# A transformer step with expert-choice routing: expert tokens picked on chip by register-addressed copies instead of gathered from DRAM

## The reference

```python
x = x + g1 * (mix @ w_out)
h2 = rms_norm(x, norm2_g) * (1 + sc2) + sh2           # modulated, sc2/sh2 differ for context and latent
x = x + g2 * expert_choice(h2, w_router, w_gate, w_up, w_down)

def expert_choice(h, w_router, w_gate, w_up, w_down):
    C = EC_FACTOR * T // N_EXPERTS                    # 64 of 512, 16 of 128
    aff = softmax(h @ w_router)
    gsel, idx = top_k(aff.T, C)                       # each expert picks its tokens
    xs = h[idx]
    hid = silu(xs @ w_gate[e]) * (xs @ w_up[e])
    ye = hid @ w_down[e] * gsel
    return zeros.at[idx].add(ye)
```

## Time and profile before

| | us |
|---|---|
| Median of three runs | 1949.23 (1947.59 to 1951.15) |
| Profiled execution: span from the first to the last instruction | 1948.8 |
| Profiled execution: its own time beside the span | not given by the page |
| TensorE busy | 1717.8 (88%) |
| VectorE busy | 630.2 (32%) |
| ScalarE busy | 327.0 (17%) |
| GpSimd busy | 139.3 (7%) |
| Mean DMA rate over the span | 274 GB/s |

### The profile page before, as it was taken

The page is one execution under the profiler, slowest core; times in us unless marked ns, Lnnn a source line. Parts: engine busy times, 40 slices in busy tenths (PEclk is TensorE's granted clock), DMA queues, the critical chain, the costliest instruction groups (busy, mean ns, idle before and its releaser), DMA issues.

```text
span 1948.8 us, 60484 instructions
## 1 busy us (share of the span) xinstructions
PE 1717.8 (88%) x28403; PEld 1357.9 (70%) x28403; DVE 630.2 (32%) x1056; ACT 327.0 (17%) x667; POOL 139.3 (7%) x169
## 2 busy tenths in 40 slices
PE   4999988967998899898969998899499999898983
PEld 2555456547998889888845444755489988898883
DVE  2399277251111111010127975832411111010112
ACT  3100156320010101010030003542110101010001
POOL 2100000100000000000010000000000000000002
PEclk9999999988999999999979999999699999999997
DMA  9246540436999999999941643033499999999995
GB/s 360 84 173 236 196 162 1 170 143 239 384 388 399 388 398 399 388 399 387 394 161 55 221 167 139 13 119 130 147 386 389 393 395 399 387 400 389 399 388 211
DMA packets 154439, 534.70 MB, mean 274 GB/s; under 512 B 5937, under 2 KB 6354, under 8 KB 154386
## 3 DMA queue, kind: packets, MB, share of 16 engines
q1 hardware_dynamic: 139600, 484.99, 64.6%
q0 software_dynamic: 12320, 42.47, 7.5%
q10 hardware_dynamic: 2466, 6.50, 0.8%
HBM read 509.30 MB, written 24.64 MB: 274 GB/s over the span
## 4 chain that ended last, share of the span: by engine, by line
PE 57%; DMA 30%; DVE 8%; SPq 2%; ACT 2%; issue 1%; POOL 0%; ACTq 0%; POOLq 0%; DVEq 0%
DMA weight_ring<-in_w_gate_dram 24%; PE ps L760 17%; PE ps L527 14%; PE ps L666 7%; PE ps L777 6%; PE ps L564 3%; DMA weight_ring<-in_w_down_dram 3%; PE ps L457 2%; DVE neg_m L1264 2%; SPq L356 2%; PE ps L626 1%; DMA weight_ring<-in_conv_w_dram 1%; PE ps L790 1%; DVE weight_ring L1300 1%; PE ps L686 1%
## 5 line engine op out<-in xcount | busy, mean ns | idle before, releaser
L760 PE MATMUL ps<-v_sb,weight_ring 128*64 128x80 f32 x16384 | 614.0, 238 | 74.9 <-DMA weight_ring<-in_w_gate_dram 51.4
L760 PEld LDWEIGHTS ps<-v_sb,weight_ring 128*64 128x64 f32 x16384 | 599.1, 141 | 93.0 <-DMA weight_ring<-in_w_gate_dram 54.7
L777 PE MATMUL ps<-mix,weight_ring 128*64 128x80 f32 x8192 | 294.3, 233 | 7.5 <-DMA weight_ring<-in_w_down_dram 4.3
L777 PEld LDWEIGHTS ps<-mix,weight_ring 128*64 128x64 f32 x8192 | 286.5, 137 | 14.5 <-issue 10.1
L527 PE MATMUL ps<-mix,weight_ring 128*128 128x512 f32 (+1 forms) x1024 | 285.1, 439 | 1.3 <-DVE mix L1158 1.0
L527 PEld LDWEIGHTS ps<-mix,weight_ring 128*128 128x128 f32 x1024 | 155.1, 193 | 130.1 <-issue 128.8
L1426 DVE TENSOR_TENSOR mix<-mix,ps 128x320 f32<-128x320 f32 x64 | 28.3, 483 | 644.5 <-PE ps L760 644.5
L1186 DVE SCALAR_TENSOR_TENSOR weight_ring<-u_gate,conv_cols,weight_ring 128x655 f32<-128x655 f32 x240 | 195.3, 887 | 0.0
L666 PE MATMUL ps<-weight_ring,mix 128*128 128x512 f32 x320 | 140.2, 592 | 0.0
L1433 DVE SCALAR_TENSOR_TENSOR qk<-ps,gsel,gate 80x1024 f32<-80x1024 f32 x32 | 41.0, 1280 | 284.7 <-PE ps L790 284.7
L1564 POOL DMA_INDIRECT x_res<-qk,row_idx x32 | 46.2, 1444 | 972.2 <-DVE qk L1433 941.2
(11 more groups left out here) (183 smaller groups left out, 1178.0 us busy)
## 6 DMA issues: line engine op xcount, KB each, us to landing
weight_ring<-in_w_gate_dram SPq DMA_DIRECT2D x64, 2048.0 KB, 23.8
weight_ring<-in_w_up_dram SPq DMA_DIRECT2D x64, 2048.0 KB
weight_ring<-in_w_down_dram SPq DMA_DIRECT2D x64, 2048.0 KB, 26.5
weight_ring<-in_w_mod_dram SPq DMA_DIRECT2D x24, 2048.0 KB, 8.2
weight_ring<-in_w_in_dram SPq DMA_DIRECT2D x10, 2048.0 KB, 12.6
weight_ring<-in_w_out_dram SPq DMA_DIRECT2D x4, 2048.0 KB, 9.2
x_res<-x_tile POOLq DMA_DIRECT2D x10, 512.0 KB, 3.3
x_unit<-x_norm ACTq DMA_DIRECT2D x10, 512.0 KB, 2.6
```

The lines of the kernel that those rows point to most:

```text
L760: last = nc.tensor.matmul(ps[c * HALF:(c + 1) * HALF, 2 * (i % 2) + f // BLK, f % BLK * CAP:(f % BLK + 1) * CAP], w[:, kk, o:o + HALF], pi ...
L777: last = nc.tensor.matmul(ps[c * HALF:(c + 1) * HALF, 4 + d // BLK, d % BLK * CAP:(d % BLK + 1) * CAP], w[:, kk, o:o + HALF], hid[:, k, :] ...
```

## The change

`x_unit` and the gathers are gone. `h2_lo` and `h2_hi` write the modulated, transposed tile into `mix` at the tile's own columns, so that after the router stage `mix` holds all 640 tokens. Each expert's 80 columns are copied from there, one token a copy (128 partitions by 8 elements), at an address held in a register: GpSimd copies tokens 0 to 39, ScalarE 40 to 79. The registers are loaded in groups of eight. For expert 0 the indices are read from the top-k tile as each round ends; for the others SP stores all indices to DRAM and loads them back as one row on partition 0. `picked_t` has two buffers. TensorE's loop is written for two experts a turn; ScalarE's is unrolled. Some waits of the router stage go with the store of `x_unit` and with the single `h2_t`. `hid`, `silu_g` and `result_t` move out of `mix`; the final norm's gain is loaded into `x_norm`.

```diff
+TOP_ROUNDS = CAP // 8
+PICK_SPLIT = 40
+PICK_LOAD = 8
...
+        picked_t = v_sb[:, 0:2 * KD * CAP].rearrange("p (b k n) -> p b k n", b=2, k=KD)
...
+        def picks_of(engine, e, at, n):
+            src = top_i[0:1, at:at + n] if e == 0 else pick_row[:, e * CAP + at:e * CAP + at + n]
+            return nc.values_load_multi_w_load_instructions(
+                src, engines=[engine], min_val=0, max_val=(N_LAT if at < CAP_LAT else N_CTX) - 1,
...
+        def picked_row(j, pick):
+            rows = mix[:, :, N_CTX:N_TOK] if j < CAP_LAT else mix[:, :, 0:N_CTX]
+            return rows[:, :, bass.ds(pick, 1)]
...  (SP, between expert 0's loads and the loop)
+                sp.wait_ge(*top_round.at(l, TOP_ROUNDS))
+                sp.dma_start(picks, top_i).then_inc(picks_stored.sem, 16)
+                sp.wait_ge(*picks_stored.at(l, 1))
+                sp.dma_start(pick_row, picks.rearrange("(a e) n -> a (e n)", a=1)).then_inc(picks_loaded.sem, 16)
...  (TensorE)
-                def picked_transposes(e):
-                    pe.wait_ge(*gathered.at(l, e + 1))
...
-                def gate_up(e):
-                    pe.wait_ge(*picked_ready.at(l, e + 1))
+                def gate_up(e, b):
+                    pe.wait_ge(*picked_lo_ready.at(l, e + 1))
+                    pe.wait_ge(*picked_hi_ready.at(l, e + 1))
...
-                    picked_transposes(e + 1)
-                    down(e)
-                    result_transposes(e)
+                with nc.Fori(0, EXPERTS // 2, engines=[mybir.EngineType.PE], hint_back_edge=True) as pair:
+                    for b in range(2):
+                        gate_up(2 * pair + b, b)
+                        pe.wait_ge(*result_taken.at(l, 2 * pair + b + 1))
+                        down(2 * pair + b)
+                        result_transposes(2 * pair + b)
...  (ScalarE)
-                        act.wait_ge(*unit_stored.at(l, i))
...
-                    act.dma_start(x_unit[tokens(OUT_TILES[i]), :], x_norm[:]).then_inc(unit_stored.sem, 16)
...
-                    if i > 0:
-                        act.wait_ge(*logits_done.at(l, i))
...
+                def pick_hi(e):
+                    for at in range(PICK_SPLIT, CAP, PICK_LOAD):
+                        if e == 0:
+                            act.wait_ge(*top_round.at(l, at // 8 + 1))
+                        elif e == 1 and at == PICK_SPLIT:
+                            act.wait_ge(*picks_loaded.at(l, 1))
+                        for j, pick in enumerate(picks_of(mybir.EngineType.Activation, e, at, PICK_LOAD), at):
+                            last = nc.scalar.activation(picked_t[:, e % 2, :, j:j + 1], picked_row(j, pick), ACT.Copy)
+                    last.then_inc(picked_hi_ready.sem, 1)
+                pick_hi(0)
+                for e in range(EXPERTS):
+                    if e + 1 < EXPERTS:
+                        pick_hi(e + 1)
...  (VectorE)
-                for dst, q, src in ((shift2_x, 3, mod[:, l]), (scale2_x, 0, scale2)):
-                    cols = src[:, q * KD:(q + 1) * KD, :]
-                    nc.vector.tensor_copy(dst[:, :, 0:CAP_LAT], cols[:, :, 1:2].to_broadcast([P, KD, CAP_LAT]))
...
-                    modulate_picked(e + 1)
...  (GpSimd)
-                gather(0)
+                pool.wait_ge(*h2_lo_ready.at(l, TILES))
+                pool.wait_ge(*h2_hi_ready.at(l, TILES))
+                pick_lo(0)
...
-                gather(1)
+                pick_lo(1)
...
-                    if e + 2 <= EXPERTS:
-                        gather(e + 2)
+                    if e + 2 < EXPERTS:
+                        pick_lo(e + 2)
```

More of the change, by code:

```diff
@@ L304, in tokens @@
             return slice(t * P, (t + 1) * P)
+        def picks_of(engine, e, at, n):
+            src = top_i[0:1, at:at + n] if e == 0 else pick_row[:, e * CAP + at:e * CAP + at + n]
+            return nc.values_load_multi_w_load_instructions(
+                src, engines=[engine], min_val=0, max_val=(N_LAT if at < CAP_LAT else N_CTX) - 1,
+                skip_runtime_bounds_check_because="max_index counts within the row that it searched")[1]
+        def picked_row(j, pick):
+            rows = mix[:, :, N_CTX:N_TOK] if j < CAP_LAT else mix[:, :, 0:N_CTX]
+            return rows[:, :, bass.ds(pick, 1)]
         def vec(t):
@@ L685, in logits @@
                     for k in range(KD):
-                        last = nc.tensor.matmul(ps[:, 6, 0:EXPERTS], h2_t[:, k, :], router[:, l, k, :],
+                        last = nc.tensor.matmul(ps[:, 6, 0:EXPERTS], mix[:, k, tokens(OUT_TILES[i])], router[:, l, k, :],
                                                 start=(k == 0), stop=(k == KD - 1))
@@ L1003, in h2_hi @@
                     act.wait_ge(*x2_transposed.at(l, i + 1))
-                    if i > 0:
-                        act.wait_ge(*logits_done.at(l, i))
                     for k in range(4, KD):
-                        last = nc.scalar.activation(h2_t[:, k, :], ps[:, 5, tokens(k - 4)], ACT.Identity,
+                        last = nc.scalar.activation(mix[:, k, tokens(OUT_TILES[i])], ps[:, 5, tokens(k - 4)], ACT.Identity,
                                                     scale=scale2[:, k, v:v + 1], bias=mod[:, l, 3 * KD + k, v:v + 1])
@@ L1334, in h2_lo @@
                     dve.wait_ge(*x2_transposed.at(l, i + 1))
-                    if i > 0:
-                        dve.wait_ge(*logits_done.at(l, i))
                     v = vec(OUT_TILES[i])
                     for k in range(4):
-                        last = nc.vector.tensor_scalar(h2_t[:, k, :], ps[:, 4, tokens(k)], scale2[:, k, v:v + 1],
+                        last = nc.vector.tensor_scalar(mix[:, k, tokens(OUT_TILES[i])], ps[:, 4, tokens(k)], scale2[:, k, v:v + 1],
                                                        mod[:, l, 3 * KD + k, v:v + 1], ALU.mult, ALU.add)
@@ L1364, in top_rounds @@
                         own(step(nc.vector.max(top_v[:, i:i + 8], left)))
-                        found = nc.vector.max_index(top_i[:, i:i + 8], top_v[:, i:i + 8], left)
+                        nc.vector.max_index(top_i[:, i:i + 8], top_v[:, i:i + 8], left).then_inc(top_round.sem, 1)
                         if r + 1 == n:
-                            own(step(found))
+                            dve.wait_ge(*top_round.at(l, i // 8 + 1))
                         else:
```

79 lines of the change are left out of this document (23 added, 56 removed).

## The result

The changed kernel takes 2116.42 us (median of 4 runs, 2108.53 to 2120.76); the kernel before, beside it, 1948.41 (4 runs, 1945.31 to 1951.15). The ratio is 1.0848, 95% interval 1.0812 to 1.0884. I had forecast 1910 with a range of 1885 to 1945: the sign was wrong, and the time lies 171 us outside.

What follows compares the result with a forecast made beforehand. The prediction took the expert loops to be bound by weight loads through saturated DMA engines. Its terms, -32 - 6 - 1.9 + 1 = -38.9 us, took 1948.8 to 1909.9, given as 1910, range 1885 to 1945.

Steps and rivals of the forecast that it cites:

- Unrolled ScalarE and GpSimd code: Instruction fetch for these two engines: as much again as the run's 0.61 MB, 1 us added, ends 0 and 3.
- the 4.3 us of slack: Expert loop: TensorE needs 29.2 of 33.5 us per expert, so removing transposes, modulating instructions and waits there gains 0.
- The rival on the slower side: Expert loop: ScalarE's picks become the bound from 23 us per expert; about 2060 us at 26; chance 16 in 100.
- Gathers out of the loop: Expert loops: 29 gathers no longer in saturated DMA time, 1.1 us each, 32 us off, ends 23 and 58.
- Rival 3: Expert loops: the gather cost nothing of its own, so removing it gains nothing; 1942 us; chance 8 in 100.
- more than half of the pair: Expert loop: gather and scatter-add together cost 2.8 us; the scatter-add, reading what it writes, should have the larger part.
- Start of the first expert: Router stage's end in each layer: picks replace gather and transposes, first expert matmul 3 us earlier, 6 us in all.
- Rival 2: Start of each layer's experts: at 1.8 us per register load only the first expert is late; 1924 us; chance 18 in 100.
- Indices through DRAM: After the router stage: SP's store and reload of the indices is hidden before the first weight slot comes free.
- Scale and shift copies: Between convolution and first row maximum: four VectorE copies on the chain disappear, 0.94 us a layer, 1.9 off.
- The sum: Whole kernel: gathers, earlier start, removed copies and added code fetch total -38.9 us, taking 1948.8 to 1909.9.
- The range: Whole kernel: 1885 to 1945 us, holding the forecast and the two milder rivals but leaving the slower case out.

Runs made afterwards that it cites:

- e3_picks_out: The changed kernel with each engine's 40 picks per expert replaced by one copy of 40 fixed columns: 2106.17 us, ratio 1.0795.
- e1_single: The changed kernel with TensorE's loop at one expert a turn and a VectorE copy of each expert's tokens into one buffer: 1902.35 us, ratio 0.9763.
- e7_single_half: e1_single with half of each weight unit loaded from expert 1 on: 1816.32 us.
- e5: e1_single with a gather of the old size put back after each of 14 scatters per layer, into a tile nothing reads: 1947.36 us, ratio 0.9972.
- e2_before_pair: The kernel before with only TensorE's expert loop written for two experts a turn, gathers kept: 2146.16 us, ratio 1.1007.
- e9_pad1: e1_single with 256 padding matmuls a turn, each with its load, in TensorE's loop, a body of about 2,070 instructions: 2455.63 us.
- e12_pad_most: e1_single with 224 padding matmuls and 224 loads a turn in TensorE's loop, a body of about 2,020 instructions: 2238.65 us.

## Why the prediction was wrong

**The step that failed** is the term for fetching code: "*Unrolled ScalarE and GpSimd code* must be fetched ... 1 us added, ends 0 and 3". It priced two engines whose code became longer. TensorE, whose loop body was written out twice, stood in the sum at nothing, and no reason was given. With it falls what was said of TensorE's time, that removed work "lies in the 4.3 us of slack: 0": with its code fetched anew TensorE takes 39.4 us an expert, over the old period of 33.5, so there is no slack.

The diff says so in one line, and the row that would have warned was among those I quoted: 0.61 MB of instructions for a kernel whose TensorE alone executes over 50,000 in its expert loops (32 x 1568) means that they were kept. At 64 bytes an instruction, 50,000 of them would have been 3.2 MB. For the two engines that the term did look at it was not too small: it allowed for 0.61 MB more, and the other instruction queue (q14), which stands at 0.48 MB against 0.13 before and 0.13 in e3_picks_out, moved 0.35 more.

The missing term was worth 210 us. The expert stage of layer 0, from the first expert matmul at 445.63 to the start of VectorE's last scaling at 1043.87, takes 598.2 us against e1_single's 504.8, and layer 1's takes 622.7 against 506.4. By the rows of the expert matmuls in the two pages, 159 of the 210 are more idle time before them and 50 are longer matmuls, at a granted clock of 0.94 and 0.96 in the two loops (e1_single: 0.99 and 0.98; e7_single_half, which waits for neither code nor weights: 1.00 in both). The miss is 206, because the rest of the sum came out somewhat better than forecast.

```profile
L768 PE MATMUL ps<-picked_now,weight_ring 128*64 128x80 f32 x16384 | 599.7, 237 | 58.0 <-DMA weight_ring<-in_w_gate_dram 39.4
L785 PE MATMUL ps<-v_sb,weight_ring 128*64 128x80 f32 x8192 | 294.2, 233 | 26.7 <-DVE v_sb L1423 19.9
```

**The rival on the slower side** had the sign but not the cause. It wanted 23 us of picks per expert; they take 5 x (0.97 + 0.47) = 7.2 us on ScalarE and 7.9 on GpSimd. e3_picks_out shows that they are not what holds TensorE.

**What held**, read from e1_single, where the failed term is taken out:
- *Gathers out of the loop.* Forecast 1.1 us each, a period of 32.4; measured 32.5 against 33.5. The two expert stages are 18.7 and 16.8 us shorter (523.5 and 523.1 before), 35.5 together against 32 forecast. Rival 3 falls. The gather that e5 puts back costs 1.6, though, not 1.0; it reads another tensor, and why it is dearer is open. That the scatter-add has more than half of the pair was not borne out: 1.5.
- *Start of the first expert.* Forecast 5.5 us after the last index, measured 3.3 with the copy and 2.7 in the changed kernel. The register load was mis-sized, 1.0 against 0.55, partly beside the copies, and a copy, 0.24 against 0.12: the gain is 5.3 to 5.9 a layer, not 3. Rival 2 falls.
- *Indices through DRAM.* Hidden, as forecast: SP was free at 444.6, the first slot at 453.1.
- *Scale and shift copies.* From the convolution's last product (its end at 257.06) to the first row maximum at 258.82 were 1.76 us in layer 0; in the changed kernel, from 254.30 to 255.11, 0.81. Forecast 0.94, measured 0.95.
- *The sum.* -38.9 forecast, 1902.35 - 1950.4 = -48.1 measured. By the two spans it is -49.5: 4.1 before the first expert, 18.7 and 16.8 in the expert stages, 8.3 between them, 1.7 at the end.
- *The range.* Its lower end, 1885, does not follow from the terms given for it: 1.4 a gather and a start 5 us earlier in each layer come to about 1898. e1_single's 1902 lies above both.

Not forecast, and open: the attention stage of layer 0, from the first row maximum to the last index, takes 187.8 us in the changed kernel and 187.7 in e1_single, against 182.2 before and 184.9 in e2_before_pair. Between 260 and 340 us the granted clock is 0.87 in the changed kernel, 0.88 in e1_single, 0.91 in e2 and 0.97 before. This eats what layer 0 gains at the start; nothing I ran isolates it.

## What to carry to other kernels

When a diff changes how many copies of a loop's body an engine's program holds, count that body in instructions as the trace counts them (here two matmuls and two loads for each float32 matmul written) before pricing anything else, and look at the instruction queue's megabytes in the profile: few for a long run means that a loop is kept and that there is something to lose. Near the limit, leave a block of 256 or more of room, for a body needs one block more or less according to where it begins, and the same body was kept in one layer and not in the other. If alternating buffers force a double body on the engine with the most instructions, a copy into one buffer on an idle engine is far cheaper: 0.5 us an expert against 7.

## What the runs showed of the hardware that I had not expected

- A TensorE body of about 3,110 instructions is fetched anew in every turn, in blocks of 256 (thirteen packets of 16.4 KB a turn), with a stop at nearly each, mostly of 0.4 to 3.3 us. A body of 1,820 is kept, and one of 2,020 is kept where it lies in eight blocks.
- The matmuls behind a long stop can run slower: behind one of 3.7 us the granted clock was 0.70, and 87 matmuls took 4.5 us in place of 3.2. Of the 210 us lost in the expert stages some 50 are longer matmuls.
- The price of a fetch depends on the other traffic: 214 us for the run with the weight queue saturated, 100 with half of the weights' bytes. In e9_pad1's last turn, when no weights are loaded any more, the only stops are two at its start (1.8 and 2.1 us) and the turn takes 42.4 us, not 51.7.
- It is dearer in layer 1 than in layer 0 in each kernel that fetches in both. Above the pace with the code kept, the changed kernel loses 8.7 and 10.9 us an expert (turn averages without the last, less 28.8), with half of the weights 1.7 and 5.5, and e9_pad1 10.2 and 14.6 (47.3 and 51.7, less 37.1, which is e12_pad_most's 35.9 and 32 matmuls more of 0.036). Why is open.
- A load of eight registers from SBUF and a copy at a register's address are cheap: 0.55 us and 0.12 us on ScalarE.
- An 80-row scatter-add of 4 KB rows costs 1.5 us of a saturated loop, an 80-row gather 1.0 (taken out) to 1.6 (put in): about equal, where I had given the scatter-add the larger part.
